# Expert weights: the remainder written over the raw tile, nine raw and five rounded tiles, and a pair's tokens transposed in halves

## What is computed

```python
def layer_forward(x, c, ...):
    mod = silu(c) @ w_ada + b_ada
    ...
    h = x * (1 + sc1) + sh1
    ... = _split_in(h @ w_in + b_in)
    ...
    mixed = (sigmoid(ga) * y_ret + sigmoid(gb) * y_fox) @ w_o
    x = layer_norm(ALPHA * x + (1 + g1) * mixed, ln1_w, ln1_b)
    h = x * (1 + sc2) + sh2
    y_moe = moe_ffn(h, w_rg, b_rg, w_re, b_re, w_e_in, w_e_out)
    return layer_norm(ALPHA * x + (1 + g2) * y_moe, ln2_w, ln2_b)

def expert_block(e, t, g):
    a, u = split(h[t] @ w_e_in[e], 2)
    return ((silu(a) * u) @ w_e_out[e]) * g
```

## Time and profile before

| | |
|---|---|
| median of 3 runs | 1226.48 us (1223.75 to 1227.85) |
| the profiled execution's own time | 1220.53 us |
| its span | 1218.5 us |
| PE busy | 1034.2 us (85%) |
| PEld busy | 771.6 us (63%) |
| DVE busy | 901.0 us (74%) |
| ACT busy | 689.4 us (57%) |
| POOL busy | 187.2 us (15%) |
| moved by DMA | 304.77 MB, mean 250 GB/s |

### The profile page before, as it was taken

The page is one execution under the profiler, slowest core; times in us unless marked ns, Lnnn a source line. Parts: engine busy times, 40 slices in busy tenths (PEclk is TensorE's granted clock), DMA queues, the critical chain, the costliest instruction groups (busy, mean ns, idle before and its releaser), DMA issues.

```text
span 1218.5 us, 12233 instructions
## 1 busy us (share of the span) xinstructions
PE 1034.2 (85%) x4643; PEld 771.6 (63%) x4643; DVE 901.0 (74%) x905; ACT 689.4 (57%) x699; POOL 187.2 (15%) x138
## 2 busy tenths in 40 slices
PE   5989999999999998986378878888889888888950
PEld 2668776778776755765366656666667666666730
DVE  6846434945546367578649998999999999998957
ACT  5622423332245456322358677888887888887832
POOL 0028102000000001541030331110111111110010
PEclk9899999999999989987569998999998999998975
DMA  9956644736647145834359889999999999999932
GB/s 341 292 114 147 164 79 131 190 112 150 208 153 182 57 152 180 287 115 179 141 180 361 321 313 339 364 382 397 379 389 352 379 379 382 385 380 398 347 106 101
DMA packets 86002, 304.77 MB, mean 250 GB/s; under 512 B 10180, under 2 KB 10228, under 8 KB 69046
## 3 DMA queue, kind: packets, MB, share of 16 engines
q1 hardware_dynamic: 74200, 278.56, 66.0%
q0 software_dynamic: 9440, 21.24, 5.5%
q10 hardware_dynamic: 2304, 4.20, 1.0%
HBM read 300.76 MB, written 14.73 MB: 259 GB/s over the span
## 4 chain that ended last, share of the span: by engine, by line
PE 46%; DVE 35%; issue 8%; ACT 8%; DMA 2%; SPq 0%; ACTq 0%; POOLq 0%; DVEq 0%
DVE w_lo L1635 23%; PE banks L1786 10%; PE banks L1792 9%; PE banks L1788 6%; PE banks L2118 5%; ACT w_hi L1001 4%; DVE w_lo L1122 2%; PE banks L2113 2%; PE banks L2125 2%; ACT w_hi L794 1%; PE banks L2105 1%; DVE y_pair L1662 1%; DMA w_raw<-in_w_ada 1%; PE banks L1814 1%; PE banks L1811 1%
## 5 line engine op out<-in xcount | busy, mean ns | idle before, releaser
L1635 DVE TENSOR_TENSOR w_lo<-w_raw,w_hi 128x2048 fp32r<-128x2048 f32 x189 | 436.9, 2336 | 30.9 <-ACT w_hi L1001 30.0
L1001 ACT ACTIVATE w_hi<-w_raw 128x2048 fp32r<-128x2048 f32 x189 | 356.1, 1906 | 16.0 <-PE banks L2118 16.0
L1122 DVE TENSOR_TENSOR w_lo<-w_raw,w_hi 128x2048 fp32r<-128x2048 f32 x71 | 164.5, 2329 | 63.4 <-ACT w_hi L794 63.4
L794 ACT ACTIVATE w_hi<-w_raw 128x2048 fp32r<-128x2048 f32 x71 | 134.5, 1910 | 125.7 <-PE banks L1792 116.2
L2118 PE MATMUL banks<-w_lo,xT_pair 128*128 128x512 f32 x512 | 156.8, 430 | 32.0 <-DVE w_lo L1635 30.9
L2113 PE MATMUL banks<-w_hi,xT_pair 128*128 128x512 f32 x512 | 151.6, 420 | 22.5 <-ACT w_hi L1001 20.0
L1786 PE MATMUL banks<-w_hi,h_hi 128*128 128x512 f32 x384 | 141.6, 409 | 7.9 <-DVE ret_qk L1156 5.2
L2118 PEld LDWEIGHTS banks<-w_lo,xT_pair 128*128 128x128 f32 x512 | 95.7, 200 | 82.1 <-DVE w_lo L1635 64.6
L2113 PEld LDWEIGHTS banks<-w_hi,xT_pair 128*128 128x128 f32 x512 | 98.1, 199 | 49.2 <-DVE xT_pair L1641 25.9
L731 POOL DMA_INDIRECT scratch_y<-y_pair,slot_row x16 | 36.0, 2251 | 471.3 <-DVE y_pair L1662 442.2
L1792 PE MATMUL banks<-w_lo,h_hi 128*128 128x512 f32 x384 | 106.1, 398 | 0.3 <-DVE w_lo L1122 0.3
(11 more groups left out here) (436 smaller groups left out, 1331.8 us busy)
## 6 DMA issues: line engine op xcount, KB each, us to landing
w_raw<-in_w_e_in SPq DMA_DIRECT2D x128, 1024.0 KB, 7.1
w_raw<-in_w_e_out SPq DMA_DIRECT2D x64, 1024.0 KB, 7.2
w_raw<-in_w_in SPq DMA_DIRECT2D x32, 1024.0 KB, 8.5
w_raw<-in_w_ada SPq DMA_DIRECT2D x24, 1024.0 KB, 6.6
bias_rows<-in_b_in ACTq DMA_DIRECT2D x16, 256.0 KB, 5.9
w_raw<-in_w_ret_proj SPq DMA_DIRECT2D x4, 1024.0 KB, 5.2
w_raw<-in_w_fox_proj SPq DMA_DIRECT2D x4, 1024.0 KB, 5.2
w_raw<-in_w_o SPq DMA_DIRECT2D x4, 1024.0 KB, 5.8
```

The costliest lines, as they stand in the source:

```text
L794: nc.scalar.activation(whi[n % NSPL][:], raw[slot_of[n]][:], ACT.Copy).then_inc(hi_done, 1)
L1001: nc.scalar.activation(whi[n % NSPL][:], raw[slot_of[n]][:], ACT.Copy).then_inc(hi_done, 1)
L1122: V.tensor_tensor(wlo[n % NSPL][:], raw[slot_of[n]][:], whi[n % NSPL][:].bitcast(F32), ALU.subtract).then_inc(lo_done, 1)
L1635: V.tensor_tensor(wlo[n % NSPL][:], raw[slot_of[n]][:], whi[n % NSPL][:].bitcast(F32), ALU.subtract).then_inc(lo_done, 1)
```

## The change

The dense weights now have six raw and four rounded tiles, the experts nine raw and five rounded ones. There are no remainder tiles any more: `w_lo` number s lies at the address of raw tile s, and DVE writes the remainder over the raw weights that it reads. So SP's load into a raw tile waits until PE has used it (`used`), not until DVE has subtracted, and ACT's rounding waits for the product four or five tiles back. The raw tiles are taken in the order in which the dense stage leaves them (`EARLY_FREE`).

The transposes of a pair's tokens are done in two halves, one in each round, through bank 7 alone: on PE behind the second input product, on ACT behind the rounding of the hidden layer, on DVE behind the hidden layer's remainder. A half waits until DVE has left the bank. Ahead of the stage five tiles are rounded and split, not three. In the router the logits of the sample tokens come before the next transposes, and the rounding of tile N0 + 1 before the last copy. `gather` counts halves, and the last loads on POOL wait for `used`.

```diff
-    NPRE, NRAW, NSPL = 4, 8, 3
+    NPRE, NRAW, HPRE, NHI = 6, 9, 4, 5
...
-    wlo = [fixed(f"w_lo{s}", [P, 4, 512], F32R) for s in range(NSPL)]
...
+    wlo = [nc.alloc_sbuf_tensor_at(f"w_lo{s}", [P, 4, 512], F32R,
+                                   offset=base + 8192 * s if s < NPRE else PH + {6: -16384, 7: -8192, 8: 61440}[s]) for s in range(NRAW)]
...
+    EARLY_FREE = (2, 3, 4, 5, 0, 1, 6, 7, 8)
+    slot_of = [n % NPRE for n in range(N0)] + [EARLY_FREE[m % NRAW] for m in range(6 * NE)]
+    hi_of = [n % HPRE for n in range(N0)] + [m % NHI for m in range(6 * NE)]
...
             if freed_at[n] is not None:
-                sp.wait_ge(lo_done, freed_at[n])
+                sp.wait_ge(used, freed_at[n])
...
             if q >= 2:
-                pool.wait_ge(x_trans, q - 1)
+                pool.wait_ge(x_trans, 2 * (q - 1))
...
-        pool.wait_ge(lo_done, tile_at[(NE - 2, 4)] + 1)
+        pool.wait_ge(used, tile_at[(NE - 1, 2)] + 1)
...
         hi(N0)
         h2T_copy(0)
+        hi(N0 + 1)
         h2T_copy(1)
-        hi(N0 + 1)
         hi(N0 + 2)
...
+        def x_high(q, half):
+
+            act.wait_ge(x_trans, 2 * q + half + 1)
+            nc.scalar.activation(xT[q % 2][:, 4 * half:4 * half + 4, :, 0:SLOTS],
+                                 bank[7][:, :].rearrange("p (k c s) -> p k c s", k=4, c=2), ACT.Copy).then_inc(x_hi, 1)
...
-        x_high(0)
+        hi(N0 + 3)
+        hi(N0 + 4)
+        x_high(0, 0)
+        x_high(0, 1)
...
             if e:
                 hidden_high(e - 1)
+            if e // 2 + 1 < PAIRS:
+                x_high(e // 2 + 1, e % 2)
+            if e:
                 item_hi(e - 1, 4)
                 item_hi(e - 1, 5)
-            if e % 2 == 0 and e + 2 < NE:
-                x_high(e // 2 + 1)
...
-            V.tensor_tensor(wlo[n % NSPL][:], raw[slot_of[n]][:], whi[n % NSPL][:].bitcast(F32), ALU.subtract).then_inc(lo_done, 1)
+            V.tensor_tensor(wlo[slot_of[n]][:], raw[slot_of[n]][:], whi[hi_of[n]][:].bitcast(F32), ALU.subtract).then_inc(lo_done, 1)
...
         h2_T(2)
+        logits(2)
         h2_T(0)
-        logits(2)
+        h2_T(1)
         logits(0)
-        h2_T(1)
         logits(1)
...
+        def x_transpose(q, half):
             pe.wait_ge(x_landed, 16 * (q + 1))
-            for k in range(KD):
-                last = tr(bank[6 + k // 4][:, P * (k % 4):P * (k % 4) + P], xg[q % 2][:, P * k:P * k + P], ident)
+            if q or half:
+                pe.wait_ge(x_split, 2 * q + half)
+            for kk in range(4):
+                k = 4 * half + kk
+                last = tr(bank[7][:, P * kk:P * kk + P], xg[q % 2][:, P * k:P * k + P], ident)
             last.then_inc(x_trans, 1)
...
             if e < NE:
-                for j in range(1, 4):
-                    in_product(j)
+                in_product(1)
+            if q + 1 < PAIRS:
+                x_transpose(q + 1, c)
+            if e < NE:
+                in_product(2)
+                in_product(3)
```

More of the change, by code:

```diff
@@ L129, in build_layer @@
     lf_tok = fixed("log_forgets", [P, 3, FH], F32)
-    raw += [fixed(f"w_raw{s}", [P, 4, 512], F32) for s in range(NPRE, 6)]
+    raw += [fixed(f"w_raw{s}", [P, 4, 512], F32) for s in range(NPRE, 8)]
     PH = off["next"]
@@ L551, in _ @@
                     expert_tile(e - 1, j)
-        sp.wait_ge(lo_done, S1)
+        sp.wait_ge(used, S1)
         sp.wait_ge(nit_ready, 1)
@@ L791, in hi @@
             act.wait_ge(raw_landed[slot_of[n]], landed[n])
-            if n >= NSPL:
-                act.wait_ge(used, n - NSPL + 1)
-            nc.scalar.activation(whi[n % NSPL][:], raw[slot_of[n]][:], ACT.Copy).then_inc(hi_done, 1)
+            if split_at[n] is not None:
+                act.wait_ge(used, split_at[n])
+            nc.scalar.activation(whi[hi_of[n]][:], raw[slot_of[n]][:], ACT.Copy).then_inc(hi_done, 1)
         def bias_rows(name):
@@ L999, in item_hi @@
             act.wait_ge(raw_landed[slot_of[n]], landed[n])
-            act.wait_ge(used, n - NSPL + 1)
-            nc.scalar.activation(whi[n % NSPL][:], raw[slot_of[n]][:], ACT.Copy).then_inc(hi_done, 1)
-        def x_high(q):
-            act.wait_ge(x_trans, q + 1)
-            for half in range(2):
-                ins = nc.scalar.activation(xT[q % 2][:, 4 * half:4 * half + 4, :, 0:SLOTS],
-                                           bank[6 + half][:, :].rearrange("p (k c s) -> p k c s", k=4, c=2), ACT.Copy)
-            ins.then_inc(x_hi, 1)
+            act.wait_ge(used, split_at[n])
+            nc.scalar.activation(whi[hi_of[n]][:], raw[slot_of[n]][:], ACT.Copy).then_inc(hi_done, 1)
+        def x_high(q, half):
+            act.wait_ge(x_trans, 2 * q + half + 1)
+            nc.scalar.activation(xT[q % 2][:, 4 * half:4 * half + 4, :, 0:SLOTS],
+                                 bank[7][:, :].rearrange("p (k c s) -> p k c s", k=4, c=2), ACT.Copy).then_inc(x_hi, 1)
         def au_rows(e):
@@ L1634, in item_lo, with x_low @@
             dve.wait_ge(hi_done, n + 1)
-            V.tensor_tensor(wlo[n % NSPL][:], raw[slot_of[n]][:], whi[n % NSPL][:].bitcast(F32), ALU.subtract).then_inc(lo_done, 1)
-        def x_low(q):
-            dve.wait_ge(x_hi, q + 1)
-            for half in range(2):
-                part = xT[q % 2][:, 4 * half:4 * half + 4]
-                ins = V.tensor_tensor(part[:, :, :, SLOTS:], bank[6 + half][:, :].rearrange("p (k c s) -> p k c s", k=4, c=2),
-                                      part[:, :, :, 0:SLOTS].bitcast(F32), ALU.subtract)
-            ins.then_inc(x_split, 1)
+            V.tensor_tensor(wlo[slot_of[n]][:], raw[slot_of[n]][:], whi[hi_of[n]][:].bitcast(F32), ALU.subtract).then_inc(lo_done, 1)
+        def x_low(q, half):
+            dve.wait_ge(x_hi, 2 * q + half + 1)
+            part = xT[q % 2][:, 4 * half:4 * half + 4]
+            V.tensor_tensor(part[:, :, :, SLOTS:], bank[7][:, :].rearrange("p (k c s) -> p k c s", k=4, c=2),
+                            part[:, :, :, 0:SLOTS].bitcast(F32), ALU.subtract).then_inc(x_split, 1)
         def hidden(e):
@@ L1791, in part @@
             for kk in range(4):
-                last = mm(b[:, :], H[:, 4 * s + kk, cols], wlo[n % NSPL][:, kk, :], start=False, stop=(s == 1 and kk == 3))
+                last = mm(b[:, :], H[:, 4 * s + kk, cols], wlo[slot_of[n]][:, kk, :], start=False, stop=(s == 1 and kk == 3))
             if t == order[2]:
@@ L2117, in split_product @@
                 for half in range(2):
-                    last = mm(bank[b + half][:, :], X[kk], wide(wlo[slot])[:, kk, 512 * half:512 * half + 512],
+                    last = mm(bank[b + half][:, :], X[kk], wide(low)[:, kk, 512 * half:512 * half + 512],
                               start=False, stop=(final and kk == 1))
```

79 lines of the change are left out of this document (41 added, 38 removed).

## The result

The changed kernel takes 1176.45 us (median of four runs, 1175.28 to 1181.35), the kernel before beside it 1225.12 (1222.34 to 1227.85): a ratio of 0.960, interval 0.958 to 0.963, or 48.7 us less. The forecast was 1193 us, a gain of 33.6. The time lies at the lower edge of the range (1176 to 1212), half a microsecond inside it.

What follows compares the result with a forecast made beforehand. VectorE (DVE) was taken to pace the expert stage, with the DMA engines close to full. Pairs 24, start 3.6, router 2 and clock 4 made 33.6 us off the 1226.48 median: 1193 us, range 1176 to 1212.

Steps and rivals of the forecast that it cites:

- The gap at the pair: Expert stage: every second expert takes 3.46 us extra as DVE, ACT and PE wait on the pair's token transposes.
- Pair: Expert stage: two experts take 32.0 us instead of 33.73, 1.7 us on each of 14 pairs, 24 us in all.
- 25-us row: Transfer rate in the profile before: 408 GB/s over 25 us, at which a pair takes 31.7 us.
- Clock: Expert stage: PE falls to 1.2 GHz after some gaps; half of four such pairs gone, 4 us, between 0 and 10.
- Start: Start of the expert stage: two added subtracts fill DVE's wait for the first tokens, gaining 3.6 us.
- Router: Router: sample tokens' logits move into PE's wait and the second tile's rounding moves up, gaining 2 us.
- Raw tiles: Expert stage: with nine tiles, 17 us are left for a load, so the later release costs nothing.
- First half: Dense half: six raw and four rounded tiles replace the old buffers at cost 0, give or take 3 us.
- best sum: Whole kernel: every term at its best end gives 47 us less, 1179 us.
- The transfers: Rival, expert stage: transfers become the bound, a pair taking 32.8 us at 395 GB/s, kernel 1207 us; chance 0.2.
- late for a half: Rival, expert stage: PE late by 1 us beyond 0.8 us of room per expert gives 28 us back, 1221; chance 0.08.
- The gathered rows: Rival, expert stage: rows landing only after 18 us cost 66 us, 1259 us; 5 us to spare; chance 0.05.

Runs made afterwards that it cites:

- e1: The kernel before with only the transposes in halves at their new places, old tiles and router kept: 1181.97 us, ratio 0.966.
- e2: The changed kernel without halves, eight transposes of a pair between the output products as before: 1217.04 us, ratio 0.994.
- e5: The changed kernel with its halves at the old places, between the output products and at the end of every round: 1245.72 us, ratio 1.016.
- e7: The kernel of halves alone with the expert remainder made for 448 of each 512 columns, so output not the reference's: 1167.93 us.
- e10: The changed kernel with the first layer norm's six operations moved from POOL to DVE behind the last sum of outputs: 1167.35 us.
- e4: The changed kernel with only three tiles rounded and split ahead of the first expert product, not five: 1178.38 us.
- e11: The changed kernel run again, unaltered, beside two later versions: 1179.86 us, ratio to before 0.963.
- e9: The changed kernel with a new order at the stage's start and POOL's six layer norm operations moved to DVE: 1165.60 us, ratio 0.952.

## Why the prediction was right, and where its sum was off

*Mechanism: right.* The gap at the pair was one piece of work handed round three standing queues. e1 and e2 put the whole gain of the steady pair on the halves, and e5 shows that halves without the new place lose.

*Pair: mis-sized, the term that was furthest off.* "I take 32.0 us, nearest to the 25-us row" should have been DVE's own sum. The pair measured 31.44, a little under the 31.56 named as the least, because DVE's half subtract costs 0.60 in the line of work and not 0.65. Fourteen pairs at 2.28 us give 31.9 us, not 24: 7.9 too little. The fear behind the 32.0 was that two near limits would cost something wherever they meet. They cost 0.06 us a pair, and e7 tells why: the transfers' own limit of 31.35 us lies under DVE's, not over it.

*Clock: half of what it gave.* Taken: 4 us, as half of four pairs at 2.5 us, which would have been 5. Outside the steady pairs the stage gains 7.6 us. 6.8 of them are the clock's: in the kernel before three later experts had lost 2.2 to 2.3 us each to it (sums 17.3 to 17.4 apart in place of 15.1). All three are gone, where half of the four counted was expected. The first pairs lose 0.8 us less; that this is the clock's too is only likely. The windows from 910 to 920 us of e2, which kept the gap, and of the change:

```profile
910.00:920.00 10.00, 7.72 (x31) 6.28 (x30) 8.51 (x6) 7.80 (x6) 0.58 (x1) 0.72 0.95 376
```

```profile
910.00:920.00 10.00, 9.84 (x52) 7.74 (x50) 10.00 (x8) 8.47 (x8) 0.00 (x0) 1.00 1.00 409
```

The falls follow the gap: three places after 740 us in before and in e2, more in e5, none in the change. The two left in the change (0.86 and 0.80 from 675 to 725 us) stand beside POOL's operations, and without these (e10) the stage has 1.00 up to 1110 us, its last 15 us apart.

*Start: size right, reason wrong.* 3.6 taken, 4.3 measured. "The two added subtracts go into the 5.32 us" is what the trace shows, but e4 shows that it is worth nothing: they come out of one wait and leave another behind. The single bank, put at 0.8 us, makes DVE wait 1.90 us for the second half. Where the 4.3 us come from is settled only in part (e1, e4).

*Router: 2 taken, 1.45 measured.* *In-place remainder: 0 taken, 0 measured* (2.27 to 2.29 us each, as before). *Raw tiles:* the slack held down to six of nine. *First half:* 0 taken, and none found in the 13 profiles; single executions lie up to 4.8 us from their mean, so a shift of 2 us would not have shown.

*Sum.* 33.6 + 7.9 + 3.6 + 0.7 - 0.55 = 45.2 us by stages, against 48.7 in the medians of the first comparison and 45.4 in that of e11 (1225.23 and 1179.86). Taken from the 1226.48 us that the prediction started from, 45.2 give 1181 us, inside the range and close to its best sum of 1179. The median of 1176.45 lies below that best sum; that it is still inside, by 0.45 us, is owed to the 3 us that the range was given under it, and is luck.

*Signs.* Named were sums 15.8 to 16.2 us apart in all experts; from the seventh on they are 15.7, ahead of that two are 20.3 (POOL's work, e9 and e10) and two 16.5 and 16.9. ACT waits for no load in the stage, and PE's wait for ACT ahead of an expert's first product, 16 times in the kernel before, is left once, at the start. That DVE would not wait for tokens but the first time did not hold: it waits 1.90 us for the first pair's second half and 7.02 for the second pair's tokens.

*Rivals.* The transfers did not bind, but by 0.1 to 0.4 us a pair only: a chance of 0.2 was not too much. They moved 411 GB/s over ten pairs and 416 when they were the limit, so the 358 GB/s for a core of the Trainium skill, page "DMA: Bandwidth & Descriptors", section "Where 436 GB/s comes from", is no bound here, with one core running. Neither PE nor ACT was late for a half (0.9 us of room). The gathered rows landed after 8.8 us, at most 10.3, where it had been 8.0 and 8.9; that is within the 5 us that they had to spare, and PE waits for them only once, at the start.

## What to carry to other kernels

Where three in-order queues stand at one small step, look first for another place for it in each queue, at which its producer is done before its consumer asks; cutting it in two without moving it made things worse, and more buffers did not help. Where the bound engine has a sum of its own and the second limit is only suspected, take that sum as the forecast and let the second limit widen the range; here it lay just under. Before crediting work that is moved into a wait, ask which wait comes behind it.
